# Moving one convolution's gate copies, opening and first tap inside the first attention

## The chip, the cores and the metric

The kernel runs on one core of one Trainium2 chip. The metric is device microseconds of that core, the median of three runs. A core has five engines that run beside one another and wait for each other through semaphores: TensorE (PE in the profile, its weight loads PEld), VectorE (DVE), ScalarE (ACT), GpSimd (POOL) and SyncE (SP), which issues the loads. Each engine works through its own instructions in the order in which the program lists them.

## The reference

Two transformer blocks in float32 over 512 tokens of width 1024. The stage that matters is the first mixer of the first block: multi-head attention with 8 heads beside a gated short convolution, both from the same projection `z`:

```
a = mla(z[..., :o1], z[..., o1:o2], z[..., o2:o3], positions, ...)
c = short_gated_conv(z[..., o3:o4], z[..., o4:o5], z[..., o5:], conv_w[i])
m = concatenate([rmsnorm(a, attn_group_norm[i]), rmsnorm(c, conv_group_norm[i])])

def short_gated_conv(b_gate, c_gate, xv, conv_w):
    u = c_gate * xv                       # "opened"
    y = conv_w[0]*u + conv_w[1]*shift(u, 1) + conv_w[2]*shift(u, 2)   # three taps
    return b_gate * y                     # "closed"
```

The attention is causal softmax attention per head. After this come the output projection, a gated feed-forward, and a second block with retention, chunked attention and two feed-forwards.

## The kernel before, in words

Every float32 product is done as three matmuls: each operand is split into a high half, rounded to a shorter type, and a low half, the rest (`three`, L730 to L734: high by high, high by low, low by high). For weights, SP loads a chunk of 128x2048 into `raw`, ScalarE copies it to the high half (`split`, L1326) and GpSimd subtracts to get the low half (`lo`, L657: four instructions of 128x512 each). There are two slots, so a chunk's load waits for the low half of the chunk two before.

Activations lie transposed, features in the partitions, tokens along the free axis. The convolution's 512 channels are done in two halves of 256. Its projections are five chunks of weights (the first half's gate is computed earlier): values of half 0, gates of half 1, values of half 1, outer gates of half 0, outer gates of half 1. Each is one group of 48 matmuls into a pair of PSUM banks.

The first attention and this convolution are woven together by hand. All engines walk the same loop over 20 "quarters" (`for quarter in range(ONE_QUARTERS + 1)`: TensorE at L964, ScalarE at L1561, VectorE at L2260). A quarter is a quarter of one convolution chunk, 12 matmuls, and five quarters hold one pair of heads: `p, phase = divmod(quarter - 1, 5)`. There are four pairs. For one pair the steps are:

- TensorE computes the scores in phases 0 and 1 (L904, L921).
- VectorE scales them, adds the mask and takes row maxima (`pair_masked`, L2188) and negates these (L2195).
- ScalarE takes exponentials in phase 1, head 0 and then head 1 (`pair_exps`, L1528, four rows of tiles a head).
- VectorE in phase 2 takes the reciprocal of the sums and scales the four tiles of each head in place (`pair_probabilities`, L2201 and L2206), in SBUF.
- TensorE transposes head 0 in phase 3 (`pair_transposes`, L934); ScalarE copies the transposed tiles to the high halves (`pair_prob_hi`, L1537), VectorE subtracts to get the low ones (`pair_prob_lo`, L2212, reading PSUM).
- In phase 4 TensorE multiplies head 0 with the values (`pair_values`, L943 and L944), which waits for the low halves, three of four first, and transposes head 1. High and low halves of head 1 follow, and its values come in the next pair's phase 0.
- ScalarE moves one half of a result to other partitions (`pair_shift`, L1545), VectorE adds (`pair_sum`, L2219).

The convolution's elementwise steps stand between these: ScalarE copies the gates out of PSUM (`conv_gate`, L1476, two copies of 128x512); VectorE multiplies them with the values in PSUM (`conv_opened`, L2228, two); GpSimd scales the product by the squared norm factor in SBUF (`conv_scaled`, L680, two); ScalarE does the first tap (`conv_first_tap`, L1551, two), VectorE the other two taps (`conv_taps`, L2239, four); VectorE closes it (`conv_closed`, L2248).

Their places before, for half 1: ScalarE copies the gates at the end of quarter 8 (second pair, phase 2), behind the split of a chunk of weights and ahead of quarter 9's high halves (L1581). VectorE opens the convolution at the end of quarter 12 (third pair, phase 1), ahead of the scalings of quarter 13 (L2287). ScalarE does the first tap at the end of quarter 13, ahead of the high halves of quarter 14 (L1583). GpSimd's own list has `conv_scaled(1)` between the low halves of the fourth and the fifth convolution chunk (L687).

Of the kernel before, what the change touches and what calls it, by code (L numbers as in the profile page):

```python
# [213 lines left out]
def build(nc, T, out):  # L214
# [3 lines left out]
    with ExitStack() as ctx:  # L218
# [52 lines left out]
        def gain(name, t):  # L271
            at = GAIN_AT[name] + t
            return gains[:, at:at + 1]
# [1046 lines left out]
        def _(act):  # L1320
            def split(c, columns=CH):

                act.wait_ge(raw_ready[c.slot], c.loads)
                if not c.early:
                    act.wait_ge(s["group_done"], c.two_before)
                act.activation(w_hi[:, c.slot, 0:columns], raw[:, c.slot, 0:columns], ACT.Copy)\  # L1326
                    .then_inc(s["w_hi_ready"], 1)

            def group_ready(g):
                act.wait_ge(s["group_done"], g.done)  # L1330
# [140 lines left out]
            def conv_gate(half):  # L1471

                g = CONV_C[half]
                group_ready(g)
                for m in range(2):
                    act.activation(conv_u[2 * half + m], ps[:, g.bank(m), :], ACT.Copy).then_inc(pair_free[g.pair], 1)  # L1476
# [46 lines left out]
            def pair_exps(a, b):  # L1523

                act.wait_ge(a.sem("nmx"), 2 * a.p + b + 1)
                for t in range(4):
                    col = slice(4 * b + t, 4 * b + t + 1)
                    act.activation(a.score_sb(b, t), a.score_sb(b, t), ACT.Exp, bias=nmx[:, col],  # L1528
                                   accum_out=sm[:, col]).then_inc(a.sem("exp"), 1)

            def pair_prob_hi(a, b):

                if a.p or b:
                    act.wait_ge(a.sem("pv"), 2 * a.p + b)
                for j, done in T_ORDER[b]:
                    act.wait_ge(a.sem("t"), 8 * a.p + 4 * b + done)
                    act.activation(a.pt(0, j), a.trans_ps(b, j), ACT.Copy).then_inc(a.sem("hi"), 1)  # L1537

            def pair_shift(a, b):

                act.wait_ge(a.sem("pv"), 2 * a.p + b + 1)
                if a.p:
                    act.wait_ge(a.sem("o"), 2 * a.p - 1 + b)
                here, there = a.rows(b), a.rows(1 - b)
                act.activation(o_shift[here, :], a.out_ps(b)[there, :], ACT.Copy).then_inc(a.sem("shift"), 1)  # L1545

            def conv_first_tap(half):

                for m in range(2):
                    act.wait_ge(s["conv_ur"], 2 * half + m + 1)  # L1550
                    act.activation(conv_y[2 * half + m], conv_u[2 * half + m], ACT.Copy,  # L1551
                                   scale=gain("conv_w", 2 * half + m)).then_inc(s["conv_tap"], 1)

            def conv_hi(half):

                for t in (2 * half, 2 * half + 1):
                    act.wait_ge(s[f"conv_out{half}"], t % 2 + 1)
                    act.activation(hn_hi[:, 4 + t, :], conv_u[t], ACT.Copy, scale=gain("conv_group_norm", t))\
                        .then_inc(s["norm_hi"], 1)

            for quarter in range(ONE_QUARTERS + 1):  # L1561
                p, phase = divmod(quarter - 1, ONE_EVERY)
                a = ONES[p]
                if quarter == ONE_QUARTERS:
                    act.wait_ge(s["conv_read"], 1)
                    conv_hi(0)
                    split(WOUT.chunk(1))
                if phase == 0 and p:
                    pair_shift(ONES[p - 1], 1)
                if phase == 1:  # L1570
                    pair_exps(a, 0)
                    pair_exps(a, 1)
                if phase == 3:
                    pair_prob_hi(a, 0)
                if phase == 4 and quarter:
                    pair_shift(a, 0)
                    pair_prob_hi(a, 1)
                if quarter in (4, 8, 12, 16):
                    n = quarter // 4 + 1
                    split(CONVS.chunk(n) if n < CONVS.chunks else WOUT.chunk(0))  # L1580
                if quarter == 8:  # L1581
                    conv_gate(1)
                if quarter in (5, 13):  # L1583
                    conv_first_tap(quarter // 13)

            conv_hi(1)
            act.wait_ge(s["one_t"], 8 * ONE_PAIRS)
# [376 lines left out]
        def _(dve):  # L1964
# [56 lines left out]
            def group_ready(g):  # L2021
                dve.wait_ge(s["group_done"], g.done)
# [160 lines left out]
            def pair_masked(a, tiles, at=MASK_AT):  # L2183

                for t, b in tiles:
                    dve.wait_ge(a.sem("s"), 8 * a.p + at[t, b])
                    col = 4 * b + t
                    dve.tensor_tensor_reduce(a.score_sb(b, t), a.score_ps(b, t), a.bias(b, t), a.scale, FMIN, ALU.add,  # L2188
                                             ALU.max, mx[:, col:col + 1]).then_inc(a.sem("mx"), 1)

            def pair_negated(a, b):

                dve.wait_ge(a.sem("mx"), 8 * a.p + a.negated[b])
                four = slice(4 * b, 4 * b + 4)
                dve.tensor_scalar(nmx[:, four], mx[:, four], -1.0, None, ALU.mult).then_inc(a.sem("nmx"), 1)  # L2195

            def pair_probabilities(a, b):

                four = slice(4 * b, 4 * b + 4)
                dve.wait_ge(a.sem("exp"), 8 * a.p + 4 * b + 4)  # L2200
                dve.reciprocal(rs[:, four], sm[:, four]).then_inc(a.sem("rs"), 1)  # L2201
                dve.wait_ge(a.sem("rs"), 2 * a.p + b + 1)
                for t in range(4):
                    col = 4 * b + t
                    score = a.score_sb(b, t)
                    dve.tensor_scalar(score, score, rs[:, col:col + 1], None, ALU.mult).then_inc(a.sem("p"), 1)  # L2206
# [8 lines left out]
            def pair_sum(a, b):  # L2215

                here = a.rows(b)
                dve.wait_ge(a.sem("shift"), 2 * a.p + b + 1)
                dve.tensor_tensor(a.summed(b), a.out_ps(b)[here, :], o_shift[here, :], ALU.add).then_inc(a.sem("o"), 1)  # L2219

            def conv_opened(half):

                xv, cg = CONV_X[half], CONV_C[half]
                group_ready(xv)
                for m in range(2):
                    dve.wait_ge(pair_free[cg.pair], cg.freed(m))
                    u = conv_u[2 * half + m]
                    dve.tensor_tensor(u, ps[:, xv.bank(m), :], u, ALU.mult).then_inc(pair_free[xv.pair], 1)  # L2228
# [31 lines left out]
            for quarter in range(ONE_QUARTERS + 1):  # L2260
                p, phase = divmod(quarter - 1, ONE_EVERY)
                a = ONES[p]
                if phase == 0:
                    pair_masked(a, ((3, 0), (3, 1)))
                    if p:
                        pair_sum(ONES[p - 1], 1)
                if phase == 1:
                    for b in range(2):
                        pair_masked(a, ((2, b), (0, b), (1, b)))
                        pair_negated(a, b)  # L2270
                if phase == 2:
                    pair_probabilities(a, 0)
                    pair_probabilities(a, 1)
                if phase == 3:
                    pair_prob_lo(a, 0)
                if quarter == ONE_QUARTERS:
                    conv_lo(0)
                    conv_closed(1)
                    for m in range(2):
                        dve.wait_ge(pair_free[CONV_B[1].pair], CONV_B[1].freed(m))  # L2280
                        dve.tensor_tensor(conv_u[2 + m], conv_u[2 + m], rstd[:, :], ALU.mult).then_inc(s["conv_out1"], 1)
                if phase == 4 and quarter:
                    pair_prob_lo(a, 1)
                    if quarter == ONE_QUARTERS:
                        conv_lo(1)
                    pair_sum(a, 0)
                if quarter in (4, 12):  # L2287
                    conv_opened(quarter // 12)
                if quarter in (6, 14):
                    conv_taps(quarter // 14)  # L2290
                if quarter == 16:
                    conv_closed(0)
# [541 lines left out]
```

## Time and profile before

| | |
|---|---|
| median of 3 runs | 2000.2 us (1999.51 to 2000.35) |
| the profiled execution | 1998.9 us |
| its span, first to last instruction | 1997.1 us |
| TensorE busy | 1977.9 us, 99% |
| VectorE, ScalarE, GpSimd busy | 49%, 39%, 46% |
| granted TensorE clock, mean | 0.998 of full speed |

The loop of quarters lies between about 80 and 180 us of the span. A row of a timeline reads: start in us, duration in us, engine, line, operation, tile written from tiles read, shapes, count of merged instructions, and in brackets the time that the engine stood idle just before and who ended that. Merged rows run from the first one's start to the last one's end. Within a run of instructions the next one starts about 0.08 us before the one before has ended.

### The profile page before, as it was taken

Reading aid. Unit: us, or ns where it says so; the run is one execution under the profiler, and the core shown is the slowest. Engines: PE = TensorE matmul, PEld = TensorE weight load, DVE = VectorE, ACT = ScalarE, POOL = GpSimd, SP = SyncE. Lnnn points to the kernel's source line nnn. Section 1 sums busy time; section 2 is a strip of 40 time slices with the busy share of each in tenths; the row PEclk is TensorE's granted clock in tenths of the full one; section 3 lists DMA queues with packets and bytes.
Section 4 is the critical chain, followed back from the end, with each engine's and each line's share of the span. In section 5 each row is a group of like instructions: output and inputs, shape, how many; then the busy total and the mean of one; then the engine's idle time right before and its main releaser. Section 6 shows DMA issues by size and latency. Waiting matters only on the chain.

```text
span 1997.1 us, 24153 instructions
## 1 busy us (share of the span) xinstructions
PE 1977.9 (99%) x9368; PEld 1643.1 (82%) x9368; DVE 973.6 (49%) x1450; ACT 781.9 (39%) x1137; POOL 914.5 (46%) x662
## 2 busy tenths in 40 slices
PE   8999999999999999999999999999999999999998
PEld 6877878888888888888888888888888888888887
DVE  7667753432358745454555131325466783123234
ACT  7446442321235443434354132233455553223232
POOL 2333555545455344444445454555433345455452
PEclk9999999999999999999999999999999999999999
DMA  5312367375322323222222323233223222332321
GB/s 161 93 45 72 116 92 124 88 101 114 99 90 85 127 65 104 69 99 76 92 76 93 106 85 105 92 97 119 70 85 102 86 71 99 106 95 95 105 84 64
DMA packets 165552, 187.00 MB, mean 94 GB/s; under 512 B 3992, under 2 KB 152224, under 8 KB 165344
## 3 DMA queue, kind: packets, MB, share of 16 engines
q1 hardware_dynamic: 163632, 181.61, 28.3%
q10 hardware_dynamic: 1584, 3.74, 4.2%
q8 instruction: 55, 0.90, 0.2%
q0 software_dynamic: 256, 0.55, 0.1%
q14 instruction: 25, 0.20, 0.0%
HBM read 180.77 MB, written 4.72 MB: 93 GB/s over the span
## 4 chain that ended last, share of the span: by engine, by line
PE 91%; DVE 4%; ACT 2%; issue 2%; POOL 1%; DMA 1%; DVEq 0%; SPq 0%; POOLq 0%; ACTq 0%
PE ps L732 29%; PE ps L733 28%; PE ps L734 28%; PE ps L904 1%; PE ps L934 1%; POOL w_lo L657 1%; PE ps L943 1%; PE ps L944 1%; PE ps L921 1%; ACT w_hi L1326 0%; ACT scr L1528 0%; DVE scr L1970 0%; DMA freq<-in_c_freq 0%; DVE hn_lo L2468 0%; DVE x L2463 0%
## 5 line engine op out<-in xcount | busy, mean ns | idle before, releaser
L657 POOL TENSOR_TENSOR w_lo<-raw,w_hi 128x512 fp32r<-128x512 f32 x636 | 896.0, 1441 | 991.3 <-ACT w_hi L1326 991.3
L732 PE MATMUL ps<-hn_hi,w_hi 128*128 128x512 f32 x1524 | 600.4, 394 | 2.2 <-DVE hn_lo L2315 1.7
L1326 ACT ACTIVATE w_hi<-raw 128x2048 fp32r<-128x2048 f32 (+1 forms) x162 | 308.6, 1905 | 735.8 <-PE ps L734 735.7
L733 PE MATMUL ps<-hn_lo,w_hi 128*128 128x512 f32 x1524 | 593.6, 390 | 0.0
L734 PE MATMUL ps<-hn_hi,w_lo 128*128 128x512 f32 x1524 | 593.4, 389 | 0.0
L733 PE MATMUL ps<-hid_lo,w_hi 128*128 128x512 f32 x904 | 351.8, 389 | 0.0
L732 PE MATMUL ps<-hid_hi,w_hi 128*128 128x512 f32 x888 | 347.0, 391 | 0.1
L734 PE MATMUL ps<-hid_hi,w_lo 128*128 128x512 f32 x888 | 345.5, 389 | 0.0
L732 PEld LDWEIGHTS ps<-hn_hi,w_hi 128*128 128x128 f32 x1524 | 286.3, 188 | 67.5 <-issue 3.5
L734 PEld LDWEIGHTS ps<-hn_hi,w_lo 128*128 128x128 f32 x1524 | 286.2, 188 | 60.4
L733 PEld LDWEIGHTS ps<-hn_lo,w_hi 128*128 128x128 f32 x1524 | 286.3, 188 | 59.0 <-issue 1.4
L2026 DVE TENSOR_TENSOR x<-ps,x 128x512 f32<-128x512 f32 x128 | 82.4, 685 | 280.6 <-PE ps L734 280.5
L733 PEld LDWEIGHTS ps<-hid_lo,w_hi 128*128 128x128 f32 x904 | 169.7, 188 | 35.0 <-issue 0.2
L732 PEld LDWEIGHTS ps<-hid_hi,w_hi 128*128 128x128 f32 x888 | 166.7, 188 | 36.8 <-DVE hid_lo L2415 0.8
L734 PEld LDWEIGHTS ps<-hid_hi,w_lo 128*128 128x128 f32 x888 | 166.7, 188 | 34.9
L2627 DVE TENSOR_TENSOR hid_lo<-scr,hid_hi 128x512 fp32r<-128x512 f32 x64 | 101.0, 1616 | 72.1 <-ACT hid_hi L1852 72.1
L2623 DVE SCALAR_TENSOR_TENSOR scr<-ps,scr 128x512 f32<-128x512 f32 x64 | 41.2, 686 | 154.3 <-PE ps L734 145.4
L2019 DVE TENSOR_TENSOR scr<-ps,scr 128x512 f32<-128x512 f32 x42 | 27.0, 686 | 138.7 <-PE ps L734 135.3
L732 PE MATMUL ps<-w_hi,hn_hi 128*128 128x512 f32 (+1 forms) x256 | 87.0, 340 | 0.4 <-DVE scr L2543 0.4
L733 PE MATMUL ps<-w_lo,hn_hi 128*128 128x512 f32 (+1 forms) x256 | 86.0, 336 | 0.0
L734 PE MATMUL ps<-w_hi,hn_lo 128*128 128x512 f32 (+1 forms) x256 | 86.0, 336 | 0.0
L1970 DVE TENSOR_TENSOR scr<-scr 128x512 f32<-128x512 f32 x64 | 66.6, 1040 | 13.0 <-ACT scr L1346 9.3
(324 smaller groups left out, 1888.1 us busy)
## 6 DMA issues: line engine op xcount, KB each, us to landing
raw<-in_mlp_w SPq DMA_DIRECT2D x64, 1024.0 KB, 5.2
raw<-in_ret_w_in SPq DMA_DIRECT2D x24, 1024.0 KB, 5.2
raw<-in_att_w_in SPq DMA_DIRECT2D x12, 1024.0 KB, 5.1
raw<-in_w_gate SPq DMA_DIRECT2D x11, 1024.0 KB, 5.3
raw<-in_w_up SPq DMA_DIRECT2D x11, 1024.0 KB, 5.3
raw<-in_w_down SPq DMA_DIRECT2D x8, 1024.0 KB, 7.9
raw<-in_ret_w_out SPq DMA_DIRECT2D x8, 1024.0 KB, 5.1
raw<-in_w_in SPq DMA_DIRECT2D x7, 1024.0 KB, 5.7
```

The source lines that it names most:

```text
L657: ins = pool.tensor_tensor(w_lo[:, slot, at], raw[:, slot, at], w_hi[:, slot, at].bitcast(F32), ALU.subtract)
L732: pe.matmul(o, hi, rhs_hi, start=start, stop=False, skip_group_check=True)
L733: pe.matmul(o, hi, rhs_lo, start=False, stop=False, skip_group_check=True)
L734: return pe.matmul(o, lo, rhs_hi, start=False, stop=stop, skip_group_check=True)
L904: ins = pe.matmul(a.score_ps(b, t), q[:, t * P:(t + 1) * P], k[:, 0:(t + 1) * P], start=(n == 0), stop=(n == last), skip_group_check=True)
L921: ins = pe.matmul(a.score_ps(b, t), q[:, t * P:(t + 1) * P], k[:, 0:(t + 1) * P], start=(nth == 0 and n == 0 and t != 0), stop=(nth == 1 a ...
L1326: act.activation(w_hi[:, c.slot, 0:columns], raw[:, c.slot, 0:columns], ACT.Copy)\
L1970: dve.tensor_tensor(ssq, ssq, squares[:, t % 2, :], ALU.add).then_inc(s["norm_acc"], 1)
L2019: dve.tensor_tensor(dst, ps[:, g.bank(m), :], r, ALU.mult).then_inc(pair_free[g.pair], 1)
L2026: dve.tensor_tensor(dst, ps[:, g.bank(m), :], dst, ALU.add).then_inc(pair_free[g.pair], 1)
L2623: dve.scalar_tensor_tensor(sq[:, t, :], ps[:, g.bank(t), :], 0.0, r_bc, ALU.max, ALU.mult).then_inc(pair_free[g.pair], 1)
L2627: dve.tensor_tensor(hid_lo[:, 2 * m + t, :], tmp[:, t, :], hid_hi[:, 2 * m + t, :].bitcast(F32), ALU.subtract)\
```

## The change

Three steps of the convolution's half 1 move; nothing is added or removed.

On ScalarE, the gate copies move from the end of quarter 8 to quarter 9, behind the high halves of head 0 of the second pair, and the first tap moves from the end of quarter 13 to quarter 14, behind the high halves of head 0 of the third pair. On VectorE, the opening moves from the end of quarter 12, ahead of all scalings of the third pair, into quarter 13, between the scalings of head 0 and head 1. GpSimd's, TensorE's and SP's lists stay as they are. Half 0 keeps its places.

```
@@ ScalarE
                 if phase == 3:
                     pair_prob_hi(a, 0)
+                if quarter == 9:
+                    conv_gate(1)
+                if quarter == 14:
+                    conv_first_tap(1)
                 if phase == 4 and quarter:
                     pair_shift(a, 0)
                     pair_prob_hi(a, 1)
...
-                if quarter == 8:
-                    conv_gate(1)
-                if quarter in (5, 13):
-                    conv_first_tap(quarter // 13)
+                if quarter == 5:
+                    conv_first_tap(0)
@@ VectorE
                 if phase == 2:
                     pair_probabilities(a, 0)
+                    if quarter == 13:
+                        conv_opened(1)
                     pair_probabilities(a, 1)
...
-                if quarter in (4, 12):
-                    conv_opened(quarter // 12)
+                if quarter == 4:
+                    conv_opened(0)
```

## Rows read from the trace of the kernel before

**Rows 1.** The page: busy time and share of the span, TensorE

```profile
PE 1977.9 (99%) x9368; PEld 1643.1 (82%) x9368; DVE 973.6 (49%) x1450; ACT 781.9 (39%) x1137; POOL 914.5 (46%) x662
```

**Rows 2.** Waits of TensorE, 84 us to the end: total, times, longest

```profile
PE ps L934 <- DVE scr L2206: 1.5, 2, 0.8
```

**Rows 3.** Timeline of TensorE and its weight loads, at the stalls

```profile
119.66 0.39 PE L733 MATMUL ps<-hn_lo,w_hi 128*128 128x512 f32 x1
119.89 0.39 PE L734 MATMUL ps<-hn_hi,w_lo 128*128 128x512 f32 x1
120.91 0.50 PE L943 MATMUL ps<-hid_hi 128*128 128x512 f32 x1 [0.64 <-DVE hid_lo L2212]
...
140.21 0.19 PEld L734 LDWEIGHTS ps<-hn_hi,w_lo 128*128 128x128 f32 x1
141.49 0.14 PEld L934 LDWEIGHTS ps<-ident,scr 128*128 128x128 f32 x1 [1.09 <-DVE scr L2206]
...
145.56 0.19 PEld L943 LDWEIGHTS ps<-hid_hi 128*128 128x128 f32 x1 [0.43 <-DVE hid_lo L2212]
...
151.03 0.19 PEld L943 LDWEIGHTS ps<-hid_hi 128*128 128x128 f32 x1 [0.52 <-DVE hid_lo L2212]
```

**Rows 4.** Timeline of VectorE, 107 to 173 us

```profile
107.08 2.73 DVE L2239 SCALAR_TENSOR_TENSOR aux<-o_buf,gains,aux 128x511 f32<-128x511 f32 x4
...
116.47 1.28 DVE L2206 TENSOR_SCALAR scr<-scr,small 128x128 f32<-128x128 f32 x4
119.50 1.35 DVE L2212 TENSOR_TENSOR hid_lo<-ps,hid_hi 128x512 fp32r<-128x512 f32 x3 [1.75 <-ACT hid_hi L1537]
...
137.24 1.29 DVE L2228 TENSOR_TENSOR o_buf<-ps,o_buf 128x512 f32<-128x512 f32 x2
138.68 0.72 DVE L2206 TENSOR_SCALAR scr<-scr,small 128x128 f32<-128x128 f32 x1
139.31 2.12 DVE L2206 TENSOR_SCALAR scr<-scr,small 128x256 f32<-128x256 f32 x3
...
144.16 1.35 DVE L2212 TENSOR_TENSOR hid_lo<-ps,hid_hi 128x512 fp32r<-128x512 f32 x3 [1.33 <-ACT hid_hi L1537]
146.96 1.76 DVE L2239 SCALAR_TENSOR_TENSOR tab<-o_buf,gains,tab 128x511 f32<-128x511 f32 x1
...
171.61 1.27 DVE L2281 TENSOR_TENSOR o_buf<-o_buf,rstd 128x512 f32<-128x512 f32 x2
```

**Rows 5.** Timeline of ScalarE, 117 to 145 us

```profile
117.94 1.05 ACT L1476 ACTIVATE o_buf<-ps 128x512 f32<-128x512 f32 x2
118.89 1.39 ACT L1537 ACTIVATE hid_hi<-ps 128x512 fp32r<-128x512 f32 x4
122.51 0.59 ACT L1545 ACTIVATE tab<-ps 64x512 f32<-64x512 f32 x1 [2.23 <-PE ps L944]
...
140.52 1.90 ACT L1326 ACTIVATE w_hi<-raw 128x2048 fp32r<-128x2048 f32 x1
143.55 1.38 ACT L1537 ACTIVATE hid_hi<-ps 128x512 fp32r<-128x512 f32 x4
```

**Rows 6.** Timeline of GpSimd, 99 to 175 us

```profile
99.02 5.04 POOL L657 TENSOR_TENSOR w_lo<-raw,w_hi 128x512 fp32r<-128x512 f32 x4
...
138.01 2.55 POOL L680 TENSOR_TENSOR o_buf<-o_buf,r_squared_t 128x512 f32<-128x512 f32 x2 [14.88 <-DVE o_buf L2228]
142.50 5.67 POOL L657 TENSOR_TENSOR w_lo<-raw,w_hi 128x512 fp32r<-128x512 f32 x4 [1.94 <-ACT w_hi L1326]
...
171.73 2.31 POOL L657 TENSOR_TENSOR w_lo<-raw,w_hi 128x512 fp32r<-128x512 f32 x1 [8.97 <-ACT w_hi L1326]
```

**Rows 7.** Slices: stretch, length, busy of five engines, granted clock, DMA

```profile
187.00:189.00 2.00, 0.34 (x4) 0.10 (x1) 1.89 (x3) 1.23 (x2) 0.00 (x0) 1.00 0.00 0
1987.00:1988.00 1.00, 1.00 (x7) 1.00 (x7) 0.00 (x0) 0.83 (x3) 0.00 (x0) 0.59 0.00 0
1988.00:1990.00 2.00, 2.00 (x12) 1.98 (x10) 0.91 (x3) 2.00 (x4) 0.00 (x0) 0.50 0.00 0
```

## The prediction

> **What bounds the kernel now.** I read the page first: TensorE is busy for 99% of the span [rows 1], so a microsecond counts only if TensorE stands still in it. Next the waits of TensorE from 84 us to the end. They are few; the largest that lies in this stage is for the scaled probabilities, made by VectorE [rows 2]. Then I looked those stalls up in TensorE's own timeline, and walked back along ScalarE, VectorE and GpSimd to what made them. The edits touch four stalls.
>
> S1, second pair of heads, head 0. The convolution's matmuls follow one another every 0.23 us (119.66, 119.89), so the next was due at 120.12; the values matmul came at 120.91, and took 0.50 instead of 0.39 because its weight load was not hidden [rows 3]. That is 0.79 + 0.11 = 0.90 us. It waited for the third low half (119.50 + 1.35 = 120.85) [rows 4], which waited for ScalarE: the convolution gate copies took 117.94 to 118.9, and only then came the high halves at 118.89 [rows 5].
>
> S2, third pair, the transposes of head 0: due 0.23 us after the load at 140.21, that is 140.44; they came at 141.49 [rows 3]. 1.05 us. They waited for the four scalings of head 0, which took 138.68 to 141.43 instead of the 1.28 us of the same four at 116.47 [rows 4]. Beside them ran GpSimd's two scalings of the opened convolution, 138.01 to 140.56 [rows 6]. VectorE's first scaling ended at 139.40, just after GpSimd's first (two in 2.55 us, so about 139.28); its second began at 139.31 and could not end before GpSimd's second did [rows 4, 6]. So here an SBUF-to-SBUF VectorE instruction waits until the running GpSimd instruction has ended, and they take turns.
>
> S3, same pair, the values of head 0: the load at 145.56 had stood idle 0.43 us [rows 3], against a usual gap of 0.23 - 0.19 = 0.04: 0.39 + 0.11 = 0.50 us. It waited for the low halves at 144.16 (+1.35 = 145.51), and these had waited 1.33 us for ScalarE [rows 4], which did the first tap between 142.42 and 143.55 [rows 5].
>
> S4, same pair, the values of head 1: idle 0.52 before 151.03 [rows 3], so 0.48 + 0.11 = 0.59 us, behind the convolution taps on VectorE, one of which took 1.76 us under GpSimd [rows 4].
>
> Together 0.90 + 1.05 + 0.50 + 0.59 = 3.04 us. No edit here can win more than that.
>
> **The change, part by part**, in the clock of the trace before; S1's gain is subtracted at the end.
>
> Gates behind the high halves. The high halves start at 117.94 instead of 118.89; the low halves follow 0.61 us behind (118.89 to 119.50) [rows 4, 5], so 118.55, third one done at 119.90, before TensorE's 120.12. S1 goes. The two gate copies (1.05 us) then lie at 119.3 to 120.4. ScalarE's next work, the shift, waited 2.23 us for TensorE until 122.51 [rows 5], about 0.9 earlier now, so the copies are covered with over a microsecond to spare; without that cover they would cost up to their 1.05 us. The opened convolution reads the gates only at 139.9.
>
> Opened convolution between the two heads. Head 0's scalings now start at 138.68 with GpSimd idle, and take 1.28 us: ready at 139.96, before the transposes' 140.44. S2 goes. But the two multiplications now stand at 139.88 in front of head 1's scalings. By the old spacings, GpSimd starts 0.77 us after them (137.24 to 138.01), at 140.65, and ends 2.55 us later, at 143.20; VectorE's scalings of head 1 start 1.44 us after them (137.24 to 138.68), at 141.32 [rows 4, 6]. So the collision isn't removed, it moves from head 0 to head 1. And it grows. Before, GpSimd then stood idle 1.94 us for the high half of the last convolution weights, until 142.50 [rows 6], and VectorE's third and fourth scaling ran free. Now GpSimd comes out of its scalings at 143.20 with that weight ready (ScalarE's split ends at 140.52 + 1.90 = 142.42 [rows 5]), and goes on without a gap, as at 99.02 [rows 6]. With turns, and four of its instructions in 5.04 us [rows 6], 1.26 each: head 1's second scaling ends at 143.35, GpSimd's first low part at 144.6, the third scaling at 144.8, GpSimd's second low part at 146.0, the fourth scaling at 146.4. GpSimd's fourth part ends near 148.8 (148.17 before [rows 6]); TensorE needs it only behind head 1's values (151.03), and SP's next load of weights, which waits for the same part, isn't split before the whole of the last pair's scores.
>
> The low halves of head 0 stand behind that on VectorE: 146.3, third done at 147.65, values at 147.7. TensorE, without S2, is due at 145.17 - 1.05 = 144.12 (145.13 was the end of the load before S3, 0.04 the usual gap). New S3: 3.58 + 0.11 = 3.7 us.
>
> The bounds of this, the one cost that no row shows whole: below, 0.3 us, if VectorE is never held (high halves at 142.4, low 0.61 later, third done at 144.4); above, the 3.7 us, since all four scalings are held in it. I take the upper end, as the nearest rows (138.68 and 139.31) show two scalings held one after the other.
>
> First tap behind the high halves. ScalarE does them at 142.4 and the tap at 143.7 to 145.0; its inputs are done on GpSimd at 143.20. Queued behind it is the shift, which waits for the values at 147.7 or later, so it is hidden. VectorE's taps start at 147.9, GpSimd's low part then has one instruction left, until 148.8; four free taps take 2.73 us [rows 4], so they end near 151.4; head 1's second low half is there at 152.3, before TensorE's 147.7 + (150.55 - 145.56) = 152.7. S4 goes, with 0.4 us to spare; gone too far, it costs 0.59 again or somewhat more.
>
> On the turns, the Trainium skill ("Advanced Engine Details and Errata", VectorE Performance Modes, Mode Summary) says that GpSimd and VectorE's two-port instructions share an SBUF port and block each other; S2's rows agree, with 2.75 us for 1.28. It leaves open who goes next: by turns the sum is the one below, if a VectorE run keeps the port it is rival A's.
>
> **Sum.** New stalls 3.7, old ones 3.04: +0.65 us. TensorE is the bound after that too, so the shift stays to the end. The profiled execution took 1998.9 us (span 1997.1) and would take 1999.5; the median of the runs, 2000.2, lies 1.3 above it, and I forecast that median, 2000.8 us.
>
> **Rivals.**
> A. VectorE keeps the port through its third and fourth scaling. For it: at 171.61 two VectorE instructions ran in 1.27 us while GpSimd's, started at 171.73, took 2.31 us [rows 4, 6]: there GpSimd waited for both. Against it: 139.31. Then head 1's scalings end at 144.08 (0.88 after GpSimd, as before), low halves at 144.0, values at 145.4: S3 1.4 us. GpSimd's weights run 0.7 later into the taps, so the values of head 1 come at 151.55 against 150.39 due: S4 1.27. 2.67 - 3.04 = -0.4: 1999.8 us, not slower. It decides from the point where GpSimd fails to get in after the second scaling, at 143.3.
> B. VectorE isn't held at all by the moved collision, so the change does what its order suggests: S3 0.3, but the taps meet GpSimd's four weight parts earlier, S4 about 1.8. -0.9: 1999.3 us. Only rows with GpSimd idle, as 116.47, speak for it. All four stalls gone would be 1997.2.
> C. Slower: the new 3.6 us of idle TensorE lowers its clock. In the trace the granted clock fell once, after the thin matmuls at the end: 0.59 in the slice of 1987 us and 0.50 in the two microseconds behind it, so half speed, 1.2 GHz, for at least 0.8 + 2 = 2.8 us; around the wait at 187 to 189, with TensorE busy 0.34 of 2.00 us, it stayed at 1.00 [rows 7]. 2.8 us at half speed in a TensorE-bound stretch cost 1.4 us: +2.05, 2002.3 us. It decides if the stall is as long as I forecast. The Trainium skill ("TensorE: Matmul & The Clock Gate", HAM oscillation) says that TensorE is throttled again where it waits too long for data; by it the time would be this rival's, and the row at 187 shows only that a shorter wait is spared.
>
> **Chances.** Forecast 0.5, A 0.2, B 0.1, C 0.15, anything else 0.05. A difference under 0.2%, 4.0 us, can't be told from no change here, and every case lies inside it: same 0.95, slower 0.03 for a cascade that I don't see, faster 0.02. The range, 1998.4 to 2002.8, takes in A, B and C with about 0.3 to 0.9 us on either side, as the runs before themselves lie 0.84 apart.
>
> **What would show it.** Right: no wait of TensorE near 120 us; the transposes at about 139.5 (0.9 earlier) without a wait; head 1's scalings some 5 us long instead of 1.28, alternating with GpSimd; then one wait of over 3 us for the low halves of that pair, and none for head 1. A is right if that wait is near 1.3 us and a second follows; B if head 1's scalings take 1.3 us; C if a slice near 147 us shows a granted clock under 1. I am wrong altogether if TensorE waits in another stage, or if the time moves by more than 4 us.

## The result and the profile after

The changed kernel is slower by 0.13%: 2002.55 us against 1999.43, medians of 20 runs each, ratio 1.0013 with a 95% interval of 1.0007 to 1.0018. That is inside the forecast range (1998.4 to 2002.8) and inside 0.2%, though twenty runs can tell it from nothing. The runs stand on two levels: nine between 2000.01 and 2001.03 (median 2000.57, +1.1 us) and eleven between 2002.43 and 2003.24 (median 2003.02, +3.6 us). The mean granted clock of TensorE, as a share of full speed, is on record for each of the twenty runs: 0.997 in each of the upper eleven, 0.998 or 0.999 in the lower nine. The profiled execution, 2003.04 us with a span of 2001.2, is of the upper level.

It began 1.36 us later than that of the kernel before (first scores of the first pair at 81.00 instead of 79.64), and S1 is gone, 0.91 us; so in the third pair 0.45 us are to be added to a time of before. On the page TensorE is as busy as it was:

```profile
PE 1980.0 (99%) x9368; PEld 1645.9 (82%) x9368; DVE 975.0 (49%) x1450; ACT 782.2 (39%) x1137; POOL 914.0 (46%) x662
```

The waits of TensorE from 84 us on (total, times, longest) have a new first line, for the low halves; the scaled probabilities fell from 1.5 us [rows 2] to 1.1:

```profile
PE ps L943 <- DVE hid_lo L2214: 2.8, 1, 2.8
...
PE ps L934 <- DVE scr L2208: 1.1, 2, 0.8
```

Its timeline at the places of the four stalls [rows 3]:

```profile
121.25 0.39 PE L734 MATMUL ps<-hn_hi,w_lo 128*128 128x512 f32 x1
121.48 0.39 PE L943 MATMUL ps<-hid_hi 128*128 128x512 f32 x1
...
140.88 0.40 PE L734 MATMUL ps<-hn_hi,w_lo 128*128 128x512 f32 x1
141.12 0.28 PE L934 MATMUL ps<-ident,scr 128*128 128x128 f32 x1
...
144.72 0.39 PE L734 MATMUL ps<-hn_hi,w_lo 128*128 128x512 f32 x1
147.86 0.79 PE L943 MATMUL ps<-hid_hi 128*128 128x512 f32 x1 [2.75 <-DVE hid_lo L2214]
...
155.84 0.39 PE L734 MATMUL ps<-hn_hi,w_lo 128*128 128x512 f32 x1
156.06 0.39 PE L943 MATMUL ps<-hid_hi 128*128 128x512 f32 x1
```

Three of the four follow the matmul before them after 0.22 to 0.24 us, without a wait: S1, S2 and S4 are gone. The third is the new S3: due at 144.95, it came at 147.86. It also took 0.79 us where the stalled one of before took 0.50. The slices behind it say why (stretch, length, busy time of five engines, granted clock, DMA):

```profile
145.00:147.00 2.00, 0.11 (x1) 0.00 (x0) 2.00 (x3) 0.38 (x1) 2.00 (x2) 1.00 0.00 0
147.00:149.00 2.00, 1.14 (x3) 0.95 (x4) 2.00 (x5) 0.00 (x0) 1.91 (x2) 0.61 0.00 0
149.00:151.00 2.00, 2.00 (x10) 2.00 (x9) 2.00 (x4) 0.39 (x1) 0.00 (x0) 0.50 0.49 145
151.00:155.00 4.00, 4.00 (x17) 3.48 (x16) 2.90 (x6) 1.85 (x5) 0.00 (x0) 0.59 0.55 194
```

The granted clock went to the lower of its two levels, 1.2 GHz, while TensorE waited, and stayed there for (0.39 x 2 + 0.50 x 2 + 0.41 x 4) x 2 = 6.8 us (what each slice lacks of 1.00, times its length, doubled because the lower level is half speed). What held the low halves is on VectorE (lines are two higher than before):

```profile
139.13 1.28 DVE L2208 TENSOR_SCALAR scr<-scr,small 128x128 f32<-128x128 f32 x4
140.32 1.29 DVE L2230 TENSOR_TENSOR o_buf<-ps,o_buf 128x512 f32<-128x512 f32 x2
141.72 0.73 DVE L2208 TENSOR_SCALAR scr<-scr,small 128x128 f32<-128x128 f32 x1
142.38 1.40 DVE L2208 TENSOR_SCALAR scr<-scr,small 128x256 f32<-128x256 f32 x1
143.70 1.45 DVE L2208 TENSOR_SCALAR scr<-scr,small 128x384 f32<-128x384 f32 x1
145.06 1.48 DVE L2208 TENSOR_SCALAR scr<-scr,small 128x512 f32<-128x512 f32 x1
146.47 1.34 DVE L2214 TENSOR_TENSOR hid_lo<-ps,hid_hi 128x512 fp32r<-128x512 f32 x3
```

and on GpSimd:

```profile
141.09 2.54 POOL L680 TENSOR_TENSOR o_buf<-o_buf,r_squared_t 128x512 f32<-128x512 f32 x2 [16.59 <-DVE o_buf L2230]
143.58 1.35 POOL L657 TENSOR_TENSOR w_lo<-raw,w_hi 128x512 fp32r<-128x512 f32 x1
144.89 1.38 POOL L657 TENSOR_TENSOR w_lo<-raw,w_hi 128x512 fp32r<-128x512 f32 x1
146.22 1.45 POOL L657 TENSOR_TENSOR w_lo<-raw,w_hi 128x512 fp32r<-128x512 f32 x1
```

Head 0's four scalings are back at 1.28 us [rows 4]. Head 1's take 141.72 to 146.54, 4.82 us: each ends just behind the end of a GpSimd instruction (142.4, 143.6, 144.9, 146.2), though one of them takes 0.29 to 0.48 us where GpSimd is idle (the kernel before, those from 114 and 116 us on). GpSimd went from its scalings straight into the weights at 143.58; the idle 1.94 us of before [rows 6] is gone.

### The profile page after: what moved, and what is told of

It reads as the page before. It is cut to its first block, busy times and chain, and to the rows that moved or that the text cites. A ratio compares the mean times of both kernels' runs of the same rounds, so it can differ in the third digit from the quotient of the medians.

```text
span 2001.2 us, 24153 instructions
## 1 busy us (share of the span) xinstructions
PE 1980.0 (99%) x9368; PEld 1645.9 (82%) x9368; DVE 975.0 (49%) x1450; ACT 782.2 (39%) x1137; POOL 914.0 (46%) x662
## 4 chain that ended last, share of the span: by engine, by line
PE 92%; DVE 3%; issue 2%; ACT 1%; POOL 1%; DMA 0%; SPq 0%; DVEq 0%; POOLq 0%; ACTq 0%
PE ps L732 29%; PE ps L734 29%; PE ps L733 29%; PE ps L934 1%; PE ps L904 1%; POOL w_lo L657 1%; PE ps L943 1%; PE ps L944 1%; PE ps L921 1%; DVE scr L2208 1%; ACT w_hi L1326 0%; DVE scr L1972 0%; DMA raw<-in_w_in 0%; DVE hn_lo L2472 0%; DVE x L2467 0%
```

## The experiments

The theory (T): the opened half's scalings on GpSimd now hold head 1's scalings on VectorE, TensorE waits about 2.9 us, and idle TensorE sometimes falls to half its clock. The rivals: the loss is spread over all three moves (R1); the levels are not TensorE's clock (R2); for one kernel, something outside this stage (R3).

Device times of one kernel scatter by 1.3 to 5.3 us between executions, so beside them stands a measure from one profile each: the time from the first score matmul of a pair (L904) to that of the next, and from the fourth pair's to the sum over columns behind it (L768). A pair without a stall takes 23.48 us, as the first does in every kernel, to within 0.02. Line numbers shift by two to six with the edits.

| kernel | pair 1 to 2 | 2 to 3 | 3 to 4 | 4 to sum |
|---|---|---|---|---|
| before | 23.48 | 24.40 | 24.97 | 29.32 |
| changed | 23.48 | 23.49 | 29.45 | 29.33 |
| e1 changed again | 23.49 | 23.48 | 29.37 | 29.31 |
| e2 gates only | 23.46 | 23.45 | 24.97 | 29.30 |
| e3 without gates | 23.48 | 24.37 | 28.10 | 29.35 |
| e4 filled | 23.46 | 23.48 | 26.52 | 29.34 |
| e5 GpSimd late | 23.48 | 23.47 | 25.75 | 29.29 |
| e6 opened early | 23.46 | 23.47 | 24.58 | 29.31 |
| e7 held | 23.48 | 24.36 | 31.77 | 29.31 |
| e8 taps at 16 | 23.48 | 23.47 | 23.49 | 35.42 |
| e9 taps at 15 | 23.46 | 23.48 | 23.47 | 29.33 |
| e10 as e5 | 23.47 | 23.48 | 26.77 | 30.56 |
| e11 e5 filled | 23.48 | 23.47 | 25.76 | 29.29 |

So S1 was worth 0.92 us and S2 to S4 together 1.49, in sum 2.41.

**e1, the changed kernel again.** No edit.

> The changed kernel once more, for a second profile. Theory T (the moved GpSimd scalings hold head 1's scalings on VectorE, TensorE idles about 2.9 us, and in some executions its clock then falls to half): two levels again, about 1.0 us over the kernel before where the clock holds and about 3.6 where it falls; every execution has the 2.9 us wait and the 4.8 us of head 1's scalings, whatever its level. Rival R1 (the loss is spread over all three moves): the wait near 145 us is under 2 us in some execution. Rival R2 (the levels have nothing to do with TensorE's clock): a profile of the upper level shows 1.00 around 148 us.

2001.10 us, ratio 1.0012 (1.0002 to 1.0021), runs from 1999.85 to 2003.38. On this chip there is a spread rather than two clean levels. The profiled run (2002.11) has the same 4.82 us and the same wait:

```profile
141.15 4.82 DVE L2208 TENSOR_SCALAR scr<-scr,small 128x128 f32<-128x128 f32 x4
147.29 0.80 PE L943 MATMUL ps<-hid_hi 128*128 128x512 f32 x1 [2.73 <-DVE hid_lo L2214]
```

The wait stands in both executions profiled. The slow clock is in this profile too, so it shows the upper level against R2, but not a lower one.

**e2, gates only.**

```
+                if quarter == 9:
+                    conv_gate(1)
...
-                if quarter == 8:
-                    conv_gate(1)
```

> Only the gate copies moved behind the high halves. T: the stall of 0.9 us near 121 us goes, the others stay: 0.8 to 0.9 us faster than before (ratio 0.9996), one level, clock 1.00. R1: no gain, or slower.

1998.39 us, ratio 0.9997 (0.9988 to 1.0006): as sized, but runs alone can't tell it from nothing. The table does: 23.45 instead of 24.40, all else as before. This move is a gain, against R1.

**e3, the other two moves without the gates'.** The opposite of e2: gates at quarter 8, opening at 13, first tap at 14.

> Opening and first tap moved, gates where they were. T: the stall near 121 us stays and the long wait comes: 0.9 us over the changed kernel at the same level, so about +1.9 us where the clock holds and +4.5 where it falls, head 1's scalings 4.8 us. R1: less than the changed kernel's loss.

2002.37 us, ratio 1.0017 (1.0008 to 1.0026). Both waits, the old S1 and the new S3:

```profile
121.07 0.50 PE L943 MATMUL ps<-hid_hi 128*128 128x512 f32 x1 [0.63 <-DVE hid_lo L2214]
147.54 0.50 PE L943 MATMUL ps<-hid_hi 128*128 128x512 f32 x1 [2.74 <-DVE hid_lo L2214]
```

So the loss comes from these two moves. By its runs this kernel is 1.3 us above e1, where 0.9 was expected. The matmul after the wait took 0.50 here: the clock fell later, and stayed down for about 3.4 us (0.81, 0.50 and 0.84 in the slices from 147 to 153), so pair 3 to 4 is 28.10, not 29.4.

**e4, the changed kernel with TensorE kept busy in the wait.**

```
                if phase == 4 and p >= 0:
+                    if p == 2:
+                        for _ in range(10):
+                            pe.matmul(ps[:, 7, :], ones_r[:, :], hn_hi[:, 0, :], start=True, stop=True, ...)
```

> The changed kernel with ten extra matmuls of 128x128 by 512 columns in front of the third pair's head 0 values, into a PSUM bank that is free there: they fill about 2.3 us of the 2.9 us idle time and cost nothing else. T: the clock stays at 1.00 near 148 us in all executions, one level only, about +1.0 us over the kernel before, and the spread over the runs is under 1 us. R2: two levels 2.5 us apart as without them. If the extra matmuls cost time themselves: over +1.3 us at one level.

1999.78 us, ratio 1.0005 (0.9996 to 1.0014), 1998.75 to 2001.11: 1.3 us below e1 on the same chip. The collision is there, a rest of the wait is there, and the clock holds:

```profile
140.75 4.85 DVE L2212 TENSOR_SCALAR scr<-scr,small 128x128 f32<-128x128 f32 x4
...
146.92 0.50 PE L943 MATMUL ps<-hid_hi 128*128 128x512 f32 x1 [0.49 <-DVE hid_lo L2218]
...
147.00:149.00 2.00, 2.00 (x15) 1.91 (x16) 2.00 (x3) 0.49 (x1) 1.00 (x1) 1.00 0.00 0
```

The mean granted clock of its eleven runs is 0.998 or 0.999, where four of e1's show 0.997. R2 falls. It also separates the two prices: the wait alone makes pair 3 to 4 26.52, 3.04 over a free pair; the clock adds 29.45 - 26.52 = 2.93 in the changed kernel's profile, 2.85 in e1's, and 28.10 - 26.52 = 1.58 in e3's. The spread, 2.4 us, was not under 1 us as I expected; the kernel before spread by 2.7 on that chip, leaving out one of its 33 runs, of 6038.68 us.

**e5, the collision taken away.** GpSimd starts the opened half's scalings only behind head 1's on VectorE; nothing else moves.

```
             def conv_scaled(half):
                 xv = CONV_X[half]
+                if half:
+                    pool.wait_ge(s["one_p"], 24)
```

> The changed kernel, with GpSimd's scalings of the opened half told to wait until VectorE has scaled head 1's probabilities, so that nothing is moved but the collision is taken away there. T: head 1's scalings take 1.28 us, the long wait of TensorE goes, the clock stays at 1.00; but the last weights' low parts start 2 us later and the convolution taps meet them, so that TensorE waits 1 to 2 us for head 1's low halves instead: -0.9 to +0.3 us against the kernel before, over 1.5 us below the changed kernel. R1 (the loss comes from the order on ScalarE or from the later opening itself): still 1 us or more over the kernel before.

2000.57 us, ratio 1.0008 (0.9999 to 1.0017), 1998.22 to 2002.95: 1.7 us over the kernel before. That is above the expected range (-0.9 to +0.3), and by the runs alone it is what R1 expected, though the profile agrees with T. VectorE's scalings of head 1, GpSimd's weights, one of VectorE's taps under them, and TensorE:

```profile
140.19 1.27 DVE L2210 TENSOR_SCALAR scr<-scr,small 128x128 f32<-128x128 f32 x4
...
144.05 6.79 POOL L657 TENSOR_TENSOR w_lo<-raw,w_hi 128x512 fp32r<-128x512 f32 x4
...
146.25 1.78 DVE L2243 SCALAR_TENSOR_TENSOR aux<-o_buf,gains,aux 128x510 f32<-128x510 f32 x1
...
150.71 0.50 PE L945 MATMUL ps<-hid_hi 128*128 128x512 f32 x1 [1.99 <-DVE hid_lo L2216]
```

Head 1's scalings are free, the long wait is gone; the weights run into the taps and a wait of 1.99 us came before head 1's values. By the table this execution should be 2.27 - 2.41 = -0.1 us. Five of the eleven runs lie 1.9 to 4.1 us over the kernel before, though; e10 and e11 ask why.

**e6, opened a quarter earlier.** VectorE waits for scores there (3.33 us idle at 134.78 in the kernel before), so the opening and GpSimd's scalings meet nothing.

```
-                    if quarter == 13:
-                        conv_opened(1)
...
-                if quarter == 4:
-                    conv_opened(0)
+                if quarter in (4, 11):
+                    conv_opened(quarter // 11)
```

> The changed kernel with the opening one quarter earlier than the kernel before had it, at the end of quarter 11 of VectorE's list, where VectorE waits for scores. T: GpSimd's scalings run before any probability is scaled, both heads' scalings take 1.28 us, no stall near 141 us and none before head 0's values; the taps still meet the last weights' low parts, so up to 1.7 us remain before head 1's values: -0.5 to -1.5 us against the kernel before, clock 1.00. R1: no faster than the kernel before.

1997.30 us, ratio 0.9994 (0.9985 to 1.0003). By the table 1.10 - 2.41 = -1.31 us. One wait remains, behind the taps:

```profile
139.80 1.27 DVE L2208 TENSOR_SCALAR scr<-scr,small 128x128 f32<-128x128 f32 x4
144.47 1.76 DVE L2241 SCALAR_TENSOR_TENSOR tab<-o_buf,gains,tab 128x511 f32<-128x511 f32 x1
...
149.57 0.50 PE L943 MATMUL ps<-hid_hi 128*128 128x512 f32 x1 [0.82 <-DVE hid_lo L2214]
```

**e7, the kernel before with TensorE held.** No new collision, only idle time.

```
                if phase == 4 and p >= 0:
+                    if p == 2:
+                        pe.wait_ge(s["conv"], 8)
```

> The kernel before, with TensorE's values of the third pair's head 0 told to wait until the convolution taps are done: an idle TensorE of about 4.7 us with no more collision than before. T (the clock falls for idleness alone): the wait costs about 4.3 us net, and the clock falls in every execution for about 6 us and costs 2 to 3 us more: +6 to +7.5 us. R2 (the clock, or the upper level, belongs to something of the changed order): +4.3 us, granted clock 1.00 behind the wait.

2004.69 us, ratio 1.0029 (1.0018 to 1.0039), 2004.12 to 2005.46. The clock falls behind the wait:

```profile
150.47 0.80 PE L943 MATMUL ps<-hid_hi 128*128 128x512 f32 x1 [4.50 <-DVE tab L2241]
...
149.00:151.00 2.00, 0.53 (x1) 0.50 (x2) 1.41 (x3) 0.00 (x0) 0.00 (x0) 0.59 0.64 184
151.00:155.00 4.00, 4.00 (x19) 3.84 (x17) 0.42 (x1) 1.47 (x3) 0.00 (x0) 0.50 0.51 174
```

So idleness alone does it here, behind 4.50 us. +5.8 us is just under what I expected; the profile (31.77 - 24.97 = +6.8) is inside.

**e8, opened early and the other two taps at quarter 16.**

```
-                if quarter in (6, 14):
-                    conv_taps(quarter // 14)
+                if quarter in (6, 16):
+                    conv_taps(quarter // 16)
```

> As the kernel with the opening at quarter 11, and the second and third taps of that half at quarter 16 of VectorE's list, behind head 1's low halves. T: all four stalls go, together 2.35 us (0.90, 0.82, 0.27 and 0.36 by matmul starts): -2 to -2.4 us against the kernel before, ratio 0.9989, no wait of TensorE for VectorE or ScalarE between 118 and 155 us. R1: less than 1 us won.

A miss: 2001.89 us, ratio 1.0015 (1.0006 to 1.0024). The third pair is free (23.49), but at the end of quarter 16 the taps meet the next weights on GpSimd and stand ahead of the fourth pair's scores, maxima and scalings:

```profile
153.93 1.83 DVE L2241 SCALAR_TENSOR_TENSOR aux<-o_buf,gains,aux 128x511 f32<-128x511 f32 x1
155.69 1.77 DVE L2241 SCALAR_TENSOR_TENSOR tab<-o_buf,gains,tab 128x511 f32<-128x511 f32 x1
...
PE ps L934 <- DVE scr L2208: 4.7, 2, 3.8
```

The last line is from the waits of TensorE: 3.8 us for the fourth pair's transposes. The granted clock fell in that wait too: 0.50 from 167 to 169 us, 0.68 in the two microseconds behind. It is the same mistake as the change's own, made one pair later.

**e9, taps at the end of quarter 15 instead**, in the gap between two chunks of weights.

> The kernel with the opening at quarter 11 of VectorE's list, and the second and third taps of that half one quarter later than in the changed kernel, at the end of quarter 15, behind head 1's low halves and ahead of the last pair's first scores, where GpSimd stands idle between two chunks of weights. T: between the scores of the third and of the fourth pair 23.5 us pass, as in the first pair, and 23.5 between those of the second and third: all four stalls gone, 2.4 us in sum, ratio 0.9988, clock 1.00, one level. R1: not over 1.3 us won (the kernel with the taps at quarter 14).

1997.70 us, ratio 0.9988 (0.9979 to 0.9997). No pair is over 23.48, no wait of TensorE is left between 118 and 160 us, and the steps that touch SBUF on both sides lie apart:

```profile
148.65 0.73 DVE L2241 SCALAR_TENSOR_TENSOR aux<-o_buf,gains,aux 128x511 f32<-128x511 f32 x1
...
141.74 5.04 POOL L657 TENSOR_TENSOR w_lo<-raw,w_hi 128x512 fp32r<-128x512 f32 x4 [6.85 <-ACT w_hi L1326]
152.94 5.04 POOL L657 TENSOR_TENSOR w_lo<-raw,w_hi 128x512 fp32r<-128x512 f32 x4 [6.16 <-ACT w_hi L1326]
```

The first is VectorE's first tap of four (0.73 each), the others GpSimd's weights before and behind them, at 1.26 us an instruction. This version beats the kernel before by 0.12%, 2.5 us; beside the changed kernel it was not run, but that one lay 0.13% above the kernel before.

**e10, e5 once more.** No new edit.

> The kernel with GpSimd's scalings late once more, for a second profile of it. By its first profile (25.75 us from pair three to four, 1.0 at 150 us) it should lie 0.1 us below the kernel before, while its runs lay 0.8 to 1.7 above. T: in a slow run of it the granted clock falls behind the 2 us wait near 150 us, and that run lies 2 to 3 us higher; a run with the clock at 1.00 is at or below the kernel before. R3 (something outside this stage): 1.00 here in a high run too, with the extra time elsewhere.

2000.21 us, ratio 1.0000 (0.9991 to 1.0009), 1997.89 to 2003.16. This time the profile caught the fall, behind the same wait of 2 us:

```profile
151.02 0.66 PE L945 MATMUL ps<-hid_hi 128*128 128x512 f32 x1 [1.98 <-DVE hid_lo L2216]
...
151.00:153.00 2.00, 1.98 (x7) 1.79 (x8) 1.22 (x3) 0.00 (x0) 0.15 (x1) 0.55 0.36 106
153.00:155.00 2.00, 2.00 (x11) 1.23 (x10) 0.00 (x0) 1.34 (x2) 0.00 (x0) 0.60 1.09 382
```

It costs 26.77 + 30.56 - 25.75 - 29.29 = 2.29 us against e5's profile, of which 0.4 is a new wait for the fourth pair's probabilities; the spans, 1998.6 and 1996.6, differ by 2.0, so nothing is added elsewhere. The profiled run, 2000.53 us, is none of the high ones, but the mean granted clock sorts all eleven: 0.996 or 0.997 in the four slowest (2001.41 to 2003.16), 0.998 or 0.999 in the other seven (1997.89 to 2000.53). That speaks against R3.

**e11, e5 with eight extra matmuls in front of the waiting values.** As e4's edit, but `range(8)`, into bank 2 at quarter 16, and behind a wait until that bank is free.

> The kernel with GpSimd's scalings late, and eight extra matmuls into a free PSUM bank in front of the third pair's head 1 values, where TensorE waits 2 us. T: the clock holds in all executions, and the median is 0 to 0.4 us below the kernel before, spread as narrow as that kernel's. R3: median and spread as without the extra matmuls, 0.8 us or more above it.

1999.61 us, ratio 0.9997 (0.9988 to 1.0006), 1999.05 to 2000.42: 0.6 us below the median of the kernel before and with half its spread (1998.69 to 2002.34 on that chip). With 0.17 us of wait left, pair 3 to 4 is 25.76, the same as in e5's undisturbed execution, and every run has a mean clock of 0.998 or 0.999. R3 falls.

## Why the prediction was right, and which of its sizes were off

**Right, by its steps; the number was helped by luck.** S1 went with the gates (e2, 0.9 us). S2 went. The collision moved to head 1 and took all four scalings, by turns: in the clock of before GpSimd started at 140.64 (forecast 140.65), the held scalings began at 141.27 (141.32) and ended at 146.09 (146.4). S4 went. The sum without the clock was forecast as +0.65 us and is 3.04 - 2.41 = +0.63 (e4 against the kernel before). Rivals A and B fell with the 4.82 us. The Trainium skill's rule on the shared port ("Advanced Engine Details and Errata", VectorE Performance Modes) is borne out by the 4.82 us, and by the low halves of 146.47, which read PSUM and took 1.34 us as ever while GpSimd ran.

The median, though, moved by 3.1 us where 0.65 was forecast. It lies in the range in part because the range was set around a kernel before of 2000.2 us, which measured 1999.43 beside the changed one; from 2000.2 the range allowed only 2.6 us upwards.

**Mis-sized: rival C.** I gave the falling clock a chance of 0.15 and 1.4 us, because TensorE's wait at 187 us had not lowered it [rows 7]. It came in eleven of the changed kernel's twenty runs by their level and their mean clock, and a fall cost 1.6 to 2.9 us where a profile of this or a nearly equal kernel caught it. So the likeliest case was C, at +3.6 us, not the sum without it. The price was too small as it was worked out from the end of the kernel, from 2.8 us at the low clock (3.4 with the slice behind, which shows 0.85 from 1990 to 1992 us); here the low clock lasted 6.8 us. And a wait that had spared the clock once was no bound: e5 and e10 are one kernel with one wait (1.99 and 1.98 us), and the clock held in one and fell in the other. The Trainium skill ("TensorE: Matmul & The Clock Gate", HAM oscillation) warns of idle gaps of TensorE, but of longer ones than the new S3. Here page and measurement differ, and the measurement decides: the clock fell behind waits of 1.98, 2.74 and 2.75 us.

**Mis-sized and cancelled.** S2 to S4 were each put about 0.22 us too high, because I measured how late the weight load came. Where matmuls follow one another, a load starts 0.23 us ahead of its own matmul; the stalled load started together with it. In S2 the load of 141.49 was 1.05 us late [rows 3], but its matmul, due 0.23 behind that of 140.43, came at 141.49 too, so it was only 0.83 late. In the kernel before:

```profile
140.43 0.39 PE L734 MATMUL ps<-hn_hi,w_lo 128*128 128x512 f32 x1
141.49 1.31 PE L934 MATMUL ps<-ident,scr 128*128 128x128 f32 x10 [0.67 <-DVE scr L2206]
```

By the table the four stalls are 2.41 us in sum, not 3.04. The new S3 was forecast as 3.58 us and measured 2.91 (each without the load that was not hidden). In the clock of before it was due at 144.50 instead of 144.12, by the same error (in S2 and in its own due time), and came at 147.41 instead of 147.7, because the held scalings ended 0.3 us sooner. The errors in the old stalls and in the new one took each other out in the sum; I was lucky there.

**Open.** The lower nine runs lie 1.1 us over the kernel before, where 0.63 was worked out. Shorter falls of the clock in some of them would do it, but no profile of the lower level was caught.

## What to carry to other kernels

Before a step is moved off an engine's critical stretch, look at what it releases on the others: here two VectorE multiplications let GpSimd go 2.6 us later, right into the stretch that was to be freed, and with its next work ready it held four instructions instead of two. Give SBUF-heavy GpSimd work the time in which VectorE waits or reads PSUM (e9). And price a wait of TensorE of 2 us or more with what its clock may cost behind it, which here was up to about as much again; a few idle matmuls in the wait kept the clock at 2.4 GHz and were worth 1.3 us (e4 against e1).

## What the runs showed of the hardware that was not expected

The price of a lowered clock varies between executions: 1.58 us in e3 and 2.29 in e10, where the low level lasted about 3.4 us by the slices, and 2.85 in e1 and 2.93 in the changed kernel, where it lasted 6.8, behind waits of 2.74, 1.98, 2.73 and 2.75 us. In e3 the matmul right behind the wait still ran at the full rate. VectorE's held instructions and GpSimd's take turns one by one here, even where VectorE's takes 0.29 us by itself and GpSimd's 1.3. That does not hold everywhere: at 171.61 us of the kernel before, two VectorE instructions between SBUF tiles took 1.27 us and one of GpSimd's, begun under them, took 2.31 [rows 4, 6]; why VectorE came first there is open. And GpSimd pays little in these turns, 1.35 to 1.45 us an instruction instead of 1.26, while VectorE's four go from 1.28 to 4.82.
